# Grouping the attention rounds of a two-model kernel: weight pieces in a row, then scores, turning and values behind one another

## What is computed

```python
def first_block(x, ...):
    h = rmsnorm(x, norm1_g[l]); proj = h @ w_in[l]     # x_rnn, g_rnn, dq, dk, dv, fq, fk, fv, f_logit, gates
    o_diff = diff_attention(dq, dk, dv, lam, rel_bias)   # softmax(q k / 8 + bias), two maps per head, 4 heads
    o_fox = forgetting_attention(fq, fk, fv, log_f)      # softmax(q k / 8 + decay), 8 heads
    g = sigmoid(gates + gate_b)
    x = x + (g0 * (y_rnn @ w_br_rnn) + g1 * (y_diff @ w_br_diff) + g2 * (y_fox @ w_br_fox)) @ w_out
    ...
def second_block(x, ...):
    for l in range(2):
        h = h + hybrid_mixer(rmsnorm_2(h), ...)          # 12 dilated sub-heads and 16 windowed heads, gated
        h = h + expert_choice_ffn(rmsnorm_2(h), ...)     # 16 experts, each reads its own 12 MB of weights
    return rmsnorm_2(h, norm_final)
```

## Time and profile before

| | before |
|---|---|
| median of 3 runs | 1806.93 us (1806.0 to 1807.1) |
| the profiled execution | 1806.43 us |
| its span, first to last instruction | 1804.6 us |
| PE busy | 1543.4 us (86%) |
| DVE busy | 796.8 us (44%) |
| ACT busy | 588.9 us (33%) |
| first block's attention | about 118 to 228 us |
| layer 0's attention | about 558 to 660 us |
| layer 1's attention | about 1213 to 1315 us |

### The profile page before, as it was taken

One profiled execution on the slowest core, in us unless ns is written; L12 is line 12 of the kernel. 1 busy time (PEld: TensorE's weight loads), 2 busy tenths in 40 slices (PEclk: granted clock), 3 DMA queues, 4 the chain that ended last, 5 costly groups with the idle time before them and its releaser, 6 DMA issues.

```text
span 1804.6 us, 33023 instructions
## 1 busy us (share of the span) xinstructions
PE 1543.4 (86%) x14738; PEld 1155.0 (64%) x14738; DVE 796.8 (44%) x1634; ACT 588.9 (33%) x1049; POOL 77.7 (4%) x88
## 2 busy tenths in 40 slices
PE   9999999999999999977666666999999967656565
PEld 8989998999898888533333323798796533323232
DVE  7886678887567866210101100658764201101011
ACT  6765546665454654000000000545642000000001
POOL 1030001000003101000000000001010000000000
PEclk9999999999999999987878888999999988898887
DMA  6534446545473578999999999854589999999997
GB/s 252 199 144 159 169 165 230 206 177 192 163 280 121 208 285 359 417 430 429 431 430 429 430 430 429 351 203 148 200 343 419 429 430 430 429 430 430 430 430 311
DMA packets 46413, 567.38 MB, mean 314 GB/s; under 512 B 6736, under 2 KB 7280, under 8 KB 11328
## 3 DMA queue, kind: packets, MB, share of 16 engines
q1 hardware_dynamic: 40912, 552.50, 74.7%
q0 software_dynamic: 3744, 12.03, 1.9%
q10 hardware_dynamic: 1616, 0.74, 0.1%
HBM read 564.18 MB, written 1.05 MB: 313 GB/s over the span
## 4 chain that ended last, share of the span: by engine, by line
PE 61%; DMA 35%; another core or an unknown queue 2%; DVE 1%; SPq 0%; ACT 0%; issue 0%; DVEq 0%
DMA slab<-in_slabs 35%; PE bank L622 10%; PE bank L624 10%; PE bank L623 10%; PE bank L687 8%; PE bank L1198 4%; PE bank L688 4%; PE bank L1250 3%; PE bank L1010 1%; PE bank L1268 1%; PE bank L1069 1%; PE bank L1033 1%; PE bank L1175 1%; PE bank L574 1%; PE bank L1257 0%
## 5 line engine op out<-in xcount | busy, mean ns | idle before, releaser
L1198 PE MATMUL bank<-slab,xe 128*32 128x256 f32 x4096 | 312.1, 460 | 153.3 <-DMA slab<-in_slabs 153.2
L1290 DVE TENSOR_TENSOR wl<-slab,wh 128x1024 fp32r<-128x1024 f32 (+1 forms) x286 | 345.0, 1219 | 137.1 <-ACT wh L1991 137.1
L1991 ACT ACTIVATE wh<-slab 128x1024 fp32r<-128x1024 f32 (+1 forms) x286 | 295.6, 1044 | 183.4 <-PE bank L624 142.8
L1198 PEld LDWEIGHTS bank<-slab,xe 128*32 128x32 f32 x4096 | 142.6, 127 | 303.0 <-DMA slab<-in_slabs 193.6
L622 PE MATMUL bank<-ht,wh 128*128 128x256 f32 x768 | 219.9, 286 | 0.7 <-DVE wl L1290 0.7
L623 PE MATMUL bank<-ht,wh 128*128 128x256 f32 x768 | 217.3, 283 | 0.0
L624 PE MATMUL bank<-ht,wl 128*128 128x256 f32 x768 | 217.2, 283 | 0.0
L687 PE MATMUL bank<-ht,wh 128*128 128x512 f32 x576 | 209.5, 405 | 0.0
L1250 PE MATMUL bank<-slab,ha 128*32 128x256 f32 x2048 | 143.6, 430 | 73.6 <-DMA slab<-in_slabs 71.1
L2404 ACT ACTIVATE ta<-bank 128x256 f32<-128x256 f32 x32 | 12.3, 384 | 505.7 <-PE bank L1198 505.7
L688 PE MATMUL bank<-ht,wl 128*128 128x256 f32 x576 | 161.4, 280 | 0.0
(11 more groups left out here) (391 smaller groups left out, 2357.3 us busy)
## 6 DMA issues: line engine op xcount, KB each, us to landing
slab<-in_slabs SPq DMA_DIRECT2D x250, 2048.0 KB, 47.9
slab<-in_slabs SPq DMA_DIRECT2D x22, 1024.0 KB, 10.0
bias<-in_bias POOLq DMA_DIRECT2D x32, 192.0 KB, 3.2
slab<-in_slabs SPq DMA_DIRECT2D x6, 512.0 KB, 28.1
bias<-in_bias POOLq DMA_DIRECT2D x8, 256.0 KB, 6.8
x<-in_x SPq DMA_DIRECT2D x2, 512.0 KB, 4.5
rg<-in_rg POOLq DMA_DIRECT2D x1, 1024.0 KB, 12.3
bt<-in_rel POOLq DMA_DIRECT2D x1, 768.0 KB, 5.8
```

The costliest lines, as they stand in the source:

```text
L1198: t = e.matmul(bk[bank][32 * j:32 * j + 32, 0:256], XE[:, c, :], w[:, k, 256 * j:256 * j + 256], start=(c == 0), stop=(c == 7))
L1290: e.tensor_tensor(lo, src, hi.bitcast(F32), ALU.subtract).then_inc(*dve_l.mark(p))
L1991: e.activation(hi, src, ACT.Copy).then_inc(*act_h.mark(p))
```

## The change

The order of the letters in the two strings is changed. In the first block, the third fill of a step moves ahead of scores and turning. In the layers, the second fill moves ahead of turning. Rates, units, buffers and all instructions stay the same in number.

```diff
-    sched_f = schedule(8, 32, "ffstfwv", lambda s: 3 * (s + 1))
+    sched_f = schedule(8, 32, "fffstwv", lambda s: 3 * (s + 1))
     fills_f = [[first["fq", 0] + k] for k in range(32)]
-    sched_l = schedule(12, 28, "swftfv", lambda s: 2 * (s + 1))
+    sched_l = schedule(12, 28, "swfftv", lambda s: 2 * (s + 1))
```

## The result

| | before, same runs | after |
|---|---|---|
| median of 4 runs each | 1807.0 us (1806.0 to 1808.1) | 1814.9 us (1814.8 to 1816.3) |
| the profiled execution | 1806.43 us | 1816.29 us |
| its span | 1804.6 us | 1814.5 us |

The ratio is 1.0047, 95% interval 1.0035 to 1.0058: the changed kernel is slower by 8.5 us (6.3 to 10.5). The forecast was 1812.0, 5.1 us over its own before; the direction was right. The median after lies inside the stated range of 1808.9 to 1815.3, but the two sets of before differ by 0.1: the ratio's 8.5 put on the forecast's own 1806.93 gives 1815.4, just past the range's upper end.

The account below looks back on a forecast made before the run. PE alone was taken to bound the attention stretches. First block +3.2 us and two layers of +1.0 make +5.2 on 1806.43, 1811.6; the median 0.5 higher gives 1812.0 us, range 1808.9 to 1815.3.

Parts of the forecast that it names:

- The waits of the first block: First block: PE waits 2.07 us at fill 2, 1.0 at fill 4, 0.65 more at the norm of the heads.
- Fill 2's wait: First block's start: fill 2, now in bank 7, waits 2.07 us until ACT has read fills 0 and 1.
- Fill 4's: First block: fill 4, also in bank 7, waits 1.0 us for ACT's reading of fills 2 and 3.
- The stall at the norm of the heads: First block, unit 4: PE's wait ahead of fill 26 grows by 0.65 us, bounds 0 and 1.5.
- What the change removes: Joins of turning and values: one return of 0.08 saved each, 0.56 us in the first block, 0.96 per layer.
- those rounds unchanged: Sign of being wrong: the rounds in between, forecast shorter by 0.08 us, stay as they were.
- Nothing is saved by grouping: Rival, both stretches: the 2.5 us saving is absent, so +7.7 us, 1814.6 us; chance 0.06.
- The ring of ACT and DVE: Layers' windowed rounds: the cycle between exponentials grows by 0.2 us, from 8.82 to 9.01, over five rounds.
- fill 24's wait: Layers: PE waits 1.4 us for the low half of fill 24's piece, bounds 0 and 2.
- ten savings of 0.08 earlier: Layers, fill 24: PE, earlier by 0.80 us, wants the piece at 642.06.
- The end of a layer: Layer's end, t11, v10 and v11 in a row: PE waits 0.6 us ahead of v11, bounds 0.3 and 0.9.
- Carried to the end one to one: Whole kernel: every shift of PE in the attention moves the kernel's end by the same amount.

Follow-up runs that it names:

- The other banks: Changed kernel with fills 2 and 3, 6 and 7 and so on of the first block back in bank 3: 1810.36 us, ratio 1.0020.
- the values-first order: Changed kernel with values ahead of turning in both strings, and fills 2 and 3 back in bank 3: 1817.07 us in a single run.
- the late tanh: Changed kernel with the layers' tanh of the second gate fill moved behind the values' high half: 1811.81 us in a single run.

## Why the prediction was right, and where it was wrong

**The waits of the first block: right.** Fill 2's wait was 2.07 by the sum; it is 2.01 idle, 2.17 by the starts. Fill 4's was 1.0; it is 0.92 idle and 1.08 by the starts. The stall at the norm of the heads grew by 0.56 where 0.65 was said. The other banks took the first two away, so their cause is shown, not only their size.

**"What the change removes": wrong.** The step that failed is "behind the turning the first step within the fill takes 0.20: 0.09 to get in, 0.08 to get back". The 0.20 is in the rows, but I didn't look at the step ahead of it: turning to fill took 0.03, 0.08 less than turning's own pace. The two cancel, in the first block and in the layers (1.08 and 1.09 by the joins above). The 0.08 saved at each of 31 joins is 0. The prediction's own sign of being wrong, "those rounds unchanged", is what came: 8.80 after 8.75, where 8.67 was forecast. What remains in a layer is a loss: in the kernel before, the pairs of matmuls of the fill behind turning came 0.347 us apart, and all others, now those of both fills, come 0.353 apart; over 8 pairs that is 0.05 a round, the difference of 8.75 and 8.80. Why those ran closer stays open, no run tells. The rival *Nothing is saved by grouping*, to which I gave 0.06, holds in this part; with the clock beside it and a smaller wait at fill 24 the loss came to 8.5 where that rival had 7.7. The Trainium skill (TensorEngine Tiling (Array Packing), Key Properties), by which a change of the tiling mode is what drains the array, had the saving at 0, and the trace agrees: three such changes a round before and after, none among full tiles, and a longer round where the values-first order adds one.

**Missing from the sum: the clock.** The wait of 2.07 was priced as 2.07, and what the clock does behind it was put at nothing without a reason. In fact PE was at half clock for 3.4 us soon after it, and that costs 1.5 more. The false saving is larger, 2.5 us in all, but the waits at fill 24 that it had made too long take 2 of them back; nothing takes back the clock's 1.5. The Trainium skill (TensorE: Matmul & The Clock Gate, HAM oscillation — how this bites in real kernels) describes such a thing: a wait for transfers makes the next stretch of matmuls start at half clock, in its example with waits of about 3 to 5 us. In four executions here 2.0 to 2.1 us were followed by it, and PE still had 0.2 to 0.9 us at the full clock first; between matmuls in a row, single waits of 0.9 to 1.9 us were followed by no fall.

**The ring of ACT and DVE: right; fill 24's wait: mis-sized.** Exponentials 9.01 apart were forecast, 9.03 came, and the late tanh brought them back to 8.80 and took both waits away. But the wait at fill 24 was 0.38 and 0.3, not 1.4: 0.8 of the 1.4 came from PE "ten savings of 0.08 earlier", and PE was not earlier; with rounds of 8.80 it was 0.2 later. 1.4 less 0.8 and less 0.2 is the 0.4 that came, so the ring's own part was sized well. A false saving was counted once as a gain and once, with the other sign, as a wait. In the layers these two errors nearly cancel: a saving of 0.96 and a wait of 1.4 became a loss of 0.24 or more and a wait of 0.4.

**The end of a layer: right.** 0.6 ahead of v11 was forecast, 0.5 measured.

**Carried to the end one to one: right, within what the runs can tell.** Losses by places sum to 8.4, and the ratio gives 8.5. In the six other kernels with several runs the two lie within 1.1 us of each other as well. Single executions differ by up to 2.9 us in the expert stage, so one pair of them could not have shown it.

By places, the changed kernel's 5.5 in the first block are 2.2 for fill 2, 1.5 for the clock, 1.1 for fill 4 and 0.6 at the norm of the heads, 5.4 of 5.5. Layer 0's 1.5 are, by starts, 0.45 at fill 24, 0.6 at v11 and 0.24 from unit 4's scores to unit 11's, where PE waits for nothing (the slower pace); 0.2 I can't place. The late tanh left 0.27, which fits the pace alone.

## What to carry to other kernels

Before you put work together to save switches, add up the steps across a join on both sides of it: on PE a late second step can be the end of an early first one, and then there is nothing to save. A wait of PE of about 2 us can cost more than its length, so look at the clock behind each one, and where it can't be avoided, give PE something short to do, measured so that it ends ahead of the release (here that was worth 1.5 us by places, less than the total times can tell). And where the order of letters also decides which buffer a table hands out, look at the table first: it made 4.9 of the 8.5 us here, and one line undoes it.

## What the runs showed that was not expected

- Behind idle times of PE of 2.01, 2.01 and 2.02 us (fill 2, in three executions) and 2.09 us (the norm of the heads, values first), the granted clock went to 0.50 within 1 us of the restart and stayed there for 3.4 us, each time. It cost 1.5 us at fill 2. With 1.95 us of identity matmuls in the gap it did not fall. Behind 0.92 (fill 4), 1.77 and 1.89 us (near 24 us) it did not fall either. At the kernel's start two waits of about 1 us close together were followed by half clock in one execution and not in another.
- A matmul 128x256 of a fill starts 0.12 after the one before at full clock and 0.213 at half, so the pace is not quite halved; an identity matmul of float32 128x128 takes 0.218.
- Joins among fill, turning and values cost nothing over the paces where all have the full 128*128 tile. The first fill matmul behind turning or values starts 0.08 early and is recorded 0.08 longer. Into a narrower tile a join takes 0.20 to 0.21, out of one 0.31.
